# TensorE's order in the first layer of a two-layer encoder: attention's values and scores ahead of the stream's outputs and inputs

## What is computed

```
for layer in range(DEPTH):
    h = rmsnorm(x, norm_w[layer])
    if layer % 2 == 0:
        proj = h @ ev_w_in[i]
        u, g_a, q, k, v, g_b = split_cols(proj, [...])
        a_out = s5_mixer(u, ...) * jax.nn.silu(g_a)
        b_out = swa_mixer(q, k, v, swa_sinks[i], rel_bias) * jax.nn.silu(g_b)
        mix = jnp.concatenate([a_out, b_out], axis=-1) @ ev_w_out[i]
    else:
        ...
        mix = c_out @ od_w_out[i]
    x = x + mix.astype(x.dtype)
return rmsnorm(x, final_norm)

# in s5_mixer: a diagonal scan per group of channels, then a gelu
_, states = lax.associative_scan(_s5_combine, (a, bu), axis=1)
y = jnp.real(jnp.einsum('blgp,gip->blgi', states, c_c))
g = jax.nn.gelu(y)

# in swa_mixer: per chunk, scores, a softmax with a sink, values
s = jnp.einsum('bcqhgd,bckhd->bhgcqk', qc, kb).astype(jnp.float32) * (SWA_HEAD_DIM ** -0.5)
p = jax.nn.softmax(jnp.concatenate([s, sink], axis=-1), axis=-1)[..., :-1]
o = jnp.einsum('bhgcqk,bckhd->bcqhgd', p.astype(v.dtype), vb)
```

## Time and profile before

| | us |
|---|---|
| median of 3 runs | 1693.33 (1692.9 to 1693.65) |
| the profiled execution | 1691.29 |
| its span, first to last instruction | 1689.5 |
| PE busy | 1642.0 (97%) |
| DVE busy | 821.4 (49%) |
| ACT busy | 630.6 (37%) |
| POOL busy | 278.1 (16%) |

### The profile page before, as it was taken

One profiled execution on the slowest core, in us unless ns is written; L12 is line 12 of the kernel. 1 busy time (PEld: TensorE's weight loads), 2 busy tenths in 40 slices (PEclk: granted clock), 3 DMA queues, 4 the chain that ended last, 5 costly groups with the idle time before them and its releaser, 6 DMA issues.

```text
span 1689.5 us, 22567 instructions
## 1 busy us (share of the span) xinstructions
PE 1642.0 (97%) x7898; PEld 1331.8 (79%) x7898; DVE 821.4 (49%) x1655; ACT 630.6 (37%) x1584; POOL 278.1 (16%) x500
## 2 busy tenths in 40 slices
PE   6999999999999799999999999999999999999997
PEld 5777788777777588888778888888888888878886
DVE  6744445667666474543552333333334443254443
ACT  6522334667666473232460222222222232131121
POOL 3883000000000431200000112222221221000000
PEclk9999999999999899999999999999999999999999
DMA  5566544454454956222243333323332332276663
GB/s 216 146 188 188 148 154 137 139 166 147 132 152 125 283 130 229 85 100 75 96 144 106 103 113 110 122 94 113 125 104 94 128 106 79 94 246 189 190 191 106
DMA packets 222217, 236.18 MB, mean 140 GB/s; under 512 B 53113, under 2 KB 169497, under 8 KB 222105
## 3 DMA queue, kind: packets, MB, share of 16 engines
q1 hardware_dynamic: 221528, 233.59, 43.5%
q10 hardware_dynamic: 576, 1.15, 0.2%
HBM read 140.12 MB, written 94.57 MB: 139 GB/s over the span
## 4 chain that ended last, share of the span: by engine, by line
PE 62%; DVE 1%; DMA 1%; ACT 0%; issue 0%; SPq 0%; POOLq 0%; POOL 0%; DVEq 0%; ACTq 0%
PE odd_bank L2143 29%; PE odd_bank L2299 10%; PE odd_bank L2190 10%; PE odd_bank L2169 3%; PE odd_bank L2249 2%; PE odd_bank L2246 2%; PE odd_bank L2247 2%; PE odd_bank L2228 1%; PE odd_bank L2152 1%; PE odd_bank L2204 1%; DMA scr_heads<-odd_ga_min 1%; PE odd_bank L2230 0%; PE odd_bank L2257 0%; PE odd_bank L2231 0%; PE odd_bank L2256 0%; PE odd_bank L2232 0%
## 5 line engine op out<-in xcount | busy, mean ns | idle before, releaser
L2143 PE MATMUL odd_bank<-ht_hi,odd_w_hi 128*128 128x512 f32 x768 | 318.4, 415 | 0.0
L2143 PE MATMUL odd_bank<-ht_lo,odd_w_hi 128*128 128x512 f32 x768 | 300.5, 391 | 0.0
L2143 PE MATMUL odd_bank<-ht_hi,odd_w_lo 128*128 128x512 f32 x768 | 298.8, 389 | 0.0
L1214 PE MATMUL ev_acc<-ht_hi,ev_w_hi 128*128 128x512 f32 x576 | 239.5, 416 | 2.4 <-DVE ht_lo L926 2.4
L1214 PE MATMUL ev_acc<-ht_hi,ev_w_lo 128*128 128x512 f32 x576 | 226.2, 393 | 0.0
L1214 PE MATMUL ev_acc<-ht_lo,ev_w_hi 128*128 128x512 f32 x576 | 226.2, 393 | 0.0
L1919 DVE COPY odd_stage<-odd_bank 128x512 f32<-128x512 f32 x96 | 66.4, 691 | 225.1 <-PE odd_bank L2143 225.1
L2143 PEld LDWEIGHTS odd_bank<-ht_lo,odd_w_hi 128*128 128x128 f32 x768 | 144.1, 188 | 31.8
L2143 PEld LDWEIGHTS odd_bank<-ht_hi,odd_w_hi 128*128 128x128 f32 x768 | 144.4, 188 | 29.9 <-issue 3.0
L2143 PEld LDWEIGHTS odd_bank<-ht_hi,odd_w_lo 128*128 128x128 f32 x768 | 144.7, 188 | 27.7
L1214 PEld LDWEIGHTS ev_acc<-ht_hi,ev_w_hi 128*128 128x128 f32 x576 | 108.7, 189 | 30.7 <-issue 5.5
(11 more groups left out here) (284 smaller groups left out, 2876.5 us busy)
## 6 DMA issues: line engine op xcount, KB each, us to landing
odd_gl_in<-scr_heads SPq DMA_DIRECT2D x32, 640.0 KB, 4.3
scr_heads<-odd_stage SPq DMA_DIRECT2D x64, 256.0 KB, 2.2
odd_w_raw<-od_w_in SPq DMA_DIRECT2D x24, 512.0 KB, 4.0
ev_w_raw<-ev_w_in SPq DMA_DIRECT2D x17, 512.0 KB, 6.1
ev_s_cos_sin<-scr_s_cos_sin SPq DMA_DIRECT2D x32, 256.0 KB
odd_xo_sum<-x SPq DMA_DIRECT2D x16, 512.0 KB, 3.9
scr_x<-odd_xo_sum SPq DMA_DIRECT2D x16, 512.0 KB, 2.9
scr_gla_mix<-odd_gl_out SPq DMA_DIRECT2D x32, 256.0 KB, 2.1
```

The lines of the kernel that those rows point to most:

```text
L1214: mm = pe.matmul(acc[n % 3][:], w[j][:, k, :], h[:, k, t], start=(k == 0 and r == 0), stop=(k == KT - 1 and r == 2))
L2143: mm = pe.matmul(acc[n % 4][:], w[j][:, k, :], h[:, k, t], start=(k == 0 and q == 0), stop=(k == KT - 1 and q == 2))
```

## The change

In the loop of PE over the positions, the two questions on the stream (`outputs`, then `inputs`) move behind those on `values` and `scores`. The functions themselves and the code of all other engines stay as they are.

```
                     if q is not None:
                         taps(q)
-                    i = stream_at(p, S_OUT(0))
-                    if i is not None:
-                        outputs(i)
-                    i = stream_at(p, S_IN(0))
-                    if i is not None:
-                        inputs(i)
                     if p == TB + 2:
                         distances()
...
                     c_ = chunk_at(p, 2 * A0)
                     if c_ is not None:
                         scores(c_)
+                    i = stream_at(p, S_OUT(0))
+                    if i is not None:
+                        outputs(i)
+                    i = stream_at(p, S_IN(0))
+                    if i is not None:
+                        inputs(i)
                     c_ = chunk_at(p, 2 * A0 + 3)
                     if c_ is not None:
                         turn_p(c_)
```

## The result

| | before | after |
|---|---|---|
| median of 9 runs each, in turn on one chip | 1694.42 | 1697.55 |
| lowest to highest | 1692.24 to 1697.77 | 1696.07 to 1702.1 |
| the profiled execution | 1691.29 | 1696.07 |
| its span | 1689.5 | 1694.3 |

The ratio is 1.0023, with a 95% interval of 1.0014 to 1.0031: slower by some 3.9 us, just beyond the 0.2% that such a measurement can tell from no change. Between the two profiled executions it is 4.8 us.

What follows compares the result with a forecast made beforehand. A loop through DVE's gelu output (25.83 us per six positions) was taken as the bound. Lateness of 3.33 at 136 plus 0.83 gave +4.16, taken as +4.1 on 1693.33: 1697.4, range 1692.0 to 1699.5.

Steps and rivals of the forecast that it cites:

- the loop of 25.83: Six positions, scores to scores: through DVE's and ACT's chain to DVE's gelu output and back to PE, 25.83 us.
- (a): PE where stream and chunk work meet: the 0.47 us stall before the outputs goes, covered by values and scores.
- (b): PE there: values wait about 1.5 us for ACT's copy of v, hand-over 0.10; first and alone, products come 0.94 later.
- the third rival: Chain hangs on PE's products: each of ten positions adds 0.94, cycle 26.8, 9.4 in all, 1702.7; chance 0.05.
- (c): Loop: 25.51 via the copy of v, plus 0.69 because inputs behind scores delay DVE's scan; cycle 26.20, 0.37 longer.
- (d): PE's own lateness: products 1.26 later after scores; values of 96 had waited 0.14, which that pays; chain's shift not broken.
- The sum: Scores at 82 at 309.43, nine cycles of 26.20 give +3.33 at 136, outputs +0.83: +4.16, taken as +4.1.
- position 76: First place where stream and chunk work meet, without values; only scores move; taken as 0, bounds 0.3 either way.
- No longer loop: Rival: DVE or ACT has room, so the scan's delay does not lengthen the loop; cycle 25.51, 1691.3; chance 0.16.
- Covered stall: Rival: values and scores cover PE's stall without a wait; ten positions save 0.47 each, 4.7 us, 1688.6; chance 0.05.
- Pushed chain: Rival: PE's products push the chain; each of ten positions adds 0.94, 9.4 in all, 1702.7; chance 0.05.
- The clock: Rival: PE's clock falls to half at longer waits; ten stretches at some 6.7 each, together 67, about 1760; chance 0.01.

Runs made afterwards that it cites:

- scores_first: Kernel before, but where stream and chunk work meet only scores go ahead of the stream: scores, outputs, inputs, values; 1692.46, ratio 0.9990.
- inputs_ahead: Changed kernel, but at even positions from 76 on inputs go ahead of values, scores and outputs; 1693.59, ratio 0.9997 to the kernel before.
- best_order: Kernel before, but where stream and chunk work meet the order is scores, outputs, values, inputs; 1689.70, ratio 0.9975.
- values_first: Kernel before, but where stream and chunk work meet only values go ahead of the stream: values, outputs, inputs, scores; 1705.09, ratio 1.0067.
- before_delay: Kernel before, order kept, plus one useless ACT copy of 128 x 512 ahead of `copy_turned` once each cycle; 1698.49, ratio 1.0020.
- after_delay: Changed kernel plus the same useless ACT copy of 128 x 512 at the same places; 1706.71, ratio 1.0071 to the kernel before.

## Why the prediction was right

**The reading of the kernel before** held: the loop of 25.83 was the bound, and the three orders that shortened the way around it got under it (scores_first 25.77, inputs_ahead 25.72, best_order 25.35).

**(a) and (b)** held. The outputs' wait vanished, the values' wait took its place, and the hand-over from the copy of v is the 0.10 forecast. From last product to values it is 388.55 - 387.14 = 1.41, of which 0.32 is the distance without a wait. The cost of 0.94 "first and alone" did not add up position by position, which is what the third rival said: the cycle would be 26.8.

**(c)** was the step that decided, and it held: the scan starts at scores + 3.59 (forecast 3.55), the copy of v ends at scores + 25.54 (25.51), the cycle is 26.22 (26.20). That the inputs' place is the cause was shown by moving them (25.72), and that 25.51 is the length of the loop without their lateness by lengthening ACT's part (26.02 = 25.51 + 0.51).

The traces show the same in one more way, for all orders at once. From the start of the scan at 94 to the start of the copy of v in front of 100 it takes the same 21.7 us whatever PE's order; only the way from the copy of v in front of 94 to that scan differs, and the two together are the cycle to 0.02:

| | copy of v to scan | scan to copy of v | cycle |
|---|---|---|---|
| before | 360.13 to 364.26: 4.13 | 21.70 | 25.83 |
| changed | 361.97 to 366.50: 4.53 | 21.69 | 26.22 |
| values_first | 363.77 to 369.07: 5.30 | 21.68 | 26.98 |
| scores_first | 361.37 to 365.47: 4.10 | 21.68 | 25.77 |
| inputs_ahead | 361.94 to 365.97: 4.03 | 21.69 | 25.72 |
| best_order | 360.51 to 364.15: 3.64 | 21.69 | 25.35 |

So every late scan was carried on in full, and every order won or lost between the copy of v and the scan.

**(d)** held in its narrow form: at 96 the values start at 371.12, 0.53 behind the copy of v (370.31 and 0.28), and wait for nothing. In scores_first I left this point out, and that was its miss, 0.27 in the cycle.

**The sum** ran, step by step:

| | forecast | measured, less the start's 0.70 |
|---|---|---|
| scores at 82 | 309.43 | 309.76 (310.46) |
| nine cycles | 235.80 | 236.01 |
| outputs behind the scores of 136 | +0.83 | +0.86 |
| PE behind 136, against before | +4.16 | +4.73 |
| second layer starts, against before | +4.1 | +4.80 (583.33) |

The start's 0.70 is no effect of the change: a product of inputs ahead of the attention, at 266.05, already stands at 266.75, with PE's first long wait 9.1 instead of 8.5. The term that was mis-sized is position 76. I took it at 0 with bounds of 0.3, and scores at 82 came 0.33 late. ACT's cast of weights waited for its DMA there, with the gelu square right behind it:

```profile
287.60 1.05 ACT L739 CAST ev_w_hi<-ev_w_raw 128x1024 fp32r<-128x1024 f32 x1 [4.68 <-DMA ev_w_raw<-ev_w_in]
288.55 0.38 ACT L807 ACTIVATE ev_s_gelu<-ev_bank 128x256 f32<-128x256 f32 x1
```

Before, that cast started at 286.42, so it is 1.18 later, 0.48 beyond the start's 0.70. This too is hardly an effect of the change. Counted from the product of inputs in the earlier trace rows, the cast starts at 20.37 in the kernel before, and at 20.67 to 21.08 in the seven other traces, among them 20.93 in before_delay, which has the old order at 76: the one trace from which the sum was made had it earliest. Why was not tried. A reading of mine was wrong here besides: I wrote that the inputs of 76 hardly move, and they start 0.84 later (286.55, less 0.70, instead of 285.01). That cost nothing, since ACT was behind its cast anyway. The second layer gave 0.7 back in this one execution (5.50 late at its start, 4.8 at its end). The median came out at 1697.55 against 1697.4, but part of this is luck: the kernel before measured 1.1 higher beside it than in the runs the sum was added to. The difference is what bears on the working, and it is 3.1 by the medians and 3.9 by the ratio, for a forecast of 4.1.

**The rivals.** No longer loop: excluded by 26.22. Covered stall: excluded by the ten waits. Pushed chain: excluded by the same 26.22, where it had 26.8. The clock did not fall in the profiled execution of the changed kernel; its stretches between 309 and 570 all show 1.00. But the rival was priced wrongly. I had only the long fall of 13.5 us to price it by, 6.7 each; the falls that after_delay shows cost 1.4 each. And it was nearer than I thought: 0.5 us more on ACT brought it on. One of the nine runs of the changed kernel took 1702.1 us with a mean clock of 0.993, the others 0.995 or 0.996; that this was such a fall is argued, not shown.

## What to carry to other kernels

Where two engines hand work back and forth, find the loop before pricing an edit: take one instruction, go through what releases what until its next instance, and sum the starts; waits inside a loop are paid only if they lengthen it, and a step moved behind the loop's head is paid once each cycle even if its engine has nothing to do. When an order is changed, follow the chain to every instruction in the cycle that waits for it, not only to the next place where the edit falls. What costs PE a wait can be put behind work that does not need the same release: here scores and outputs ahead of values, but inputs not so late that the scan waits.

## What the runs showed of the hardware

**Short falls of TensorE's clock.** In after_delay, behind PE waits of 1.55, 1.58 and 1.56 us, the granted clock fell for about 4 us. Two such stretches, in after_delay and in before_delay:

```profile
391.01:394.96 3.95, 3.95 (x12) 3.16 (x11) 1.89 (x6) 2.10 (x6) 0.00 (x0) 0.57 0.56 169
```

```profile
864.57:868.59 4.02, 4.02 (x14) 2.46 (x15) 1.35 (x2) 2.50 (x4) 0.00 (x0) 0.60 0.00 0
```

0.57 and 0.60 are means between 1.2 GHz (0.50) for most of the stretch and 2.4 GHz for the rest. The second is in the second layer, behind this wait, before which the same place in the kernel before is shown:

```profile
858.33 1.14 PE L2216 MATMUL odd_bank<-odd_ga_low,odd_ga_w 32*128 32x512 f32 x8 [1.43 <-DVE odd_ga_min L1932]
...
864.57 1.36 PE L2219 MATMUL odd_bank<-odd_ga_low,odd_ga_w 32*128 32x512 f32 x8 [2.09 <-DVE odd_ga_min L1935]
```

In the kernel before PE waited 1.43 at that place and in the changed one 1.09, and the clock stayed at 1.00 for the 4.02 us behind; in after_delay it waited 1.92 and the clock fell once more, to a mean of 0.57. So a part of before_delay's 2.8 us in the second layer is such a fall, at a place where no useless copy stands. Why the wait there was longer was not tried. The Trainium skill, "TensorE: Matmul & The Clock Gate", section "Part 1: The HAM clock gate", says that an idle TensorE is throttled; the trace agrees in kind, at waits of 1.55 to 2.09 us. The length of one wait does not settle it: the first three of after_delay (1.71, 1.58, 1.55) brought no fall, the fourth (1.55) did, and values_first went through ten waits of 1.33 to 1.49 at 1.00. What else decides was not tried.

**A layer's end gives a lead back.** In best_order PE finished the first layer 3.4 us earlier, and the next layer started 1.0 earlier, since its start follows the loads of the gelu results. The other 2.5 us went to the queue that issues the last store and these loads: the store took 2.33 instead of 0.33, and the loads took 7.75 instead of 7.26. The load of the DMA engines does not tell the two kernels apart: their busy share in the 2 us ahead of the store and in the 2 behind it was 1.06 and 1.05 before, and 1.02 and 1.05 in best_order. Why the store took longer stays open.
